# Two blocks on one core: the first two slabs of IN's second half of K in turns, and four visits of w_ada one chunk later

## What is computed

```python
c_act = jax.nn.silu(c)
mod = c_act @ w_ada[l] + b_ada[l]                      # 2048 x 12288
sh1, sc1, gt1, sh2, sc2, gt2 = jnp.split(mod, N_MOD, axis=-1)
h = modulate(rmsnorm(x, g_norm_mix[l]), sh1, sc1)      # h * (1 + scale) + shift
proj = h @ w_in[l]                                     # 2048 x 3072
xr, gr, xp = proj[..., :D_LRU], proj[..., D_LRU:2 * D_LRU], proj[..., 2 * D_LRU:]
```

## Time and profile before

| | |
|---|---|
| median of 3 runs | 2534.44 us (2533.34 to 2534.62) |
| the profiled execution | 2534.16 us, of which 2531.9 are its span |
| PE busy | 2494.3 us, 99% |
| DVE busy | 1833.2 us, 72% |
| ACT busy | 1182.2 us, 47% |
| granted clock of PE | 0.996 of full, mean |

### The profile page before, as it was taken

The page is one execution under the profiler, slowest core; times in us unless marked ns, Lnnn a source line. Parts: engine busy times, 40 slices in busy tenths (PEclk is TensorE's granted clock), DMA queues, the critical chain, the costliest instruction groups (busy, mean ns, idle before and its releaser), DMA issues.

```text
span 2531.9 us, 42099 instructions
## 1 busy us (share of the span) xinstructions
PE 2494.3 (99%) x15684; PEld 2173.4 (86%) x15684; DVE 1833.2 (72%) x2377; ACT 1182.2 (47%) x1442; POOL 17.6 (1%) x52
## 2 busy tenths in 40 slices
PE   7999999999999999999999999999999999999998
PEld 6888888888888888888888888888888888888887
DVE  5678989996556655787685665676788668875886
ACT  3355445544444444654454554455544444444444
POOL 0000000000000000000000000000000000000000
PEclk9999999999999999999999999999999999999999
DMA  9999978787666665566555555565555655565554
GB/s 392 410 375 362 371 261 276 248 330 240 187 187 187 190 205 170 180 207 192 181 167 174 159 184 190 182 195 189 180 193 184 196 178 182 196 197 181 186 172 127
DMA packets 165174, 554.68 MB, mean 219 GB/s; under 512 B 16560, under 2 KB 20656, under 8 KB 165056
## 3 DMA queue, kind: packets, MB, share of 16 engines
q1 hardware_dynamic: 163728, 549.85, 65.2%
q0 software_dynamic: 1328, 3.21, 0.4%
HBM read 550.37 MB, written 2.10 MB: 218 GB/s over the span
## 4 chain that ended last, share of the span: by engine, by line
PE 87%; DVE 7%; DMA 2%; issue 2%; ACT 2%; SPq 0%; DVEq 0%; ACTq 0%
PE ps L642 51%; PE ps L649 25%; PE ps L639 2%; DMA ride<-in_w_ada 2%; DVE split L1377 2%; PE pm L667 1%; DVE acc_ada L1443 1%; PE ps L646 1%; PE ps L622 1%; PE ps L623 1%; PE ps L624 1%; ACT split L1010 1%; DVE x_t L1543 0%; DVE val L1397 0%; DVE ssq L1461 0%
## 5 line engine op out<-in xcount | busy, mean ns | idle before, releaser
L1377 DVE TENSOR_TENSOR split<-raw,split 128x1024 fp32r<-128x1024 f32 (+1 forms) x864 | 1030.8, 1204 | 591.8 <-ACT split L1010 587.3
L1010 ACT ACTIVATE split<-raw 128x1024 fp32r<-128x1024 f32 (+1 forms) x864 | 897.0, 1044 | 1069.7 <-PE ps L649 940.5
L642 PE MATMUL ps<-h_s,split 128*128 128x512 f32 x3592 | 1134.2, 397 | 4.5 <-DVE h_s L1521 2.5
L649 PEld LDWEIGHTS ps<-h_s,split 128*128 128x128 f32 x3592 | 675.7, 188 | 159.9
L642 PE MATMUL ps<-mid_s,split 128*128 128x512 f32 x2336 | 735.0, 396 | 0.8 <-DVE split L1377 0.4
L649 PE MATMUL ps<-h_s,split 128*128 128x256 f32 x3592 | 706.5, 278 | 0.0
L642 PEld LDWEIGHTS ps<-h_s,split 128*128 128x128 f32 x3592 | 548.6, 189 | 9.3 <-issue 5.6
L649 PEld LDWEIGHTS ps<-mid_s,split 128*128 128x128 f32 x2336 | 438.8, 188 | 103.8
L649 PE MATMUL ps<-mid_s,split 128*128 128x256 f32 x2336 | 459.0, 278 | 0.0
L642 PEld LDWEIGHTS ps<-mid_s,split 128*128 128x128 f32 x2336 | 355.6, 189 | 4.7 <-issue 2.7
L1017 ACT ACTIVATE low<-ps 128x512 f32<-128x512 f32 x238 | 138.1, 580 | 22.3 <-PE ps L649 22.3
(11 more groups left out here) (285 smaller groups left out, 1482.9 us busy)
## 6 DMA issues: line engine op xcount, KB each, us to landing
raw<-in_w_in SPq DMA_DIRECT2D x224, 512.0 KB, 3.8
raw<-in_w_ffn_down SPq DMA_DIRECT2D x128, 512.0 KB, 4.2
ride<-in_w_ada SPq DMA_DIRECT2D x46, 1024.0 KB, 11.5
raw<-in_w_ffn_gate SPq DMA_DIRECT2D x88, 512.0 KB, 4.1
raw<-in_w_ffn_up SPq DMA_DIRECT2D x88, 512.0 KB, 4.3
raw<-in_w_ffn_a SPq DMA_DIRECT2D x88, 512.0 KB, 3.6
raw<-in_w_ffn_b SPq DMA_DIRECT2D x88, 512.0 KB, 4.5
raw<-in_w_out SPq DMA_DIRECT2D x64, 512.0 KB, 4.5
```

The source lines that it names most:

```text
L642: pe.matmul(ps[:, s, b, :], split[:, slot, k, 0, b * P:(b + 1) * P], acts[:, k0 + k, :, :].rearrange("p h t -> p (h t)"), start=start, sto ...
L649: mm = pe.matmul(ps[:, s, b, 0:T], split[:, slot, k, 1, b * P:(b + 1) * P], acts[:, k0 + k, 0, :], start=False, stop=stop)
L1010: act.activation(split[:, c, 0:kt, 0, :], raw[:, CHUNKS * s + c, 0:kt, :], ACT.Copy).then_inc(hi_ready, 1)
L1377: dve.tensor_tensor(split[:, c, 0:kt, 1, :], raw[:, CHUNKS * s + c, 0:kt, :], split[:, c, 0:kt, 0, :].bitcast(F32), ALU.subtract).then_inc ...
```

## The change

Three things change. `_early` swaps slab and quarter for the first four chunks of the second half: chunk 24 is quarter 2 of slab 0, 25 quarter 2 of slab 1, 26 quarter 3 of slab 0, 27 quarter 3 of slab 1. PE multiplies them so (`first_halves`), with both PSUM places open at once, and DVE's evacuation of slab 0 waits for 27 used chunks, not 26. In `_rides` the visits after chunks 16, 18, 20 and 21 come after 17, 19, 21 and 22, and with them their loads, DVE's and ACT's steps on unit 3, and nothing else.

```diff
 def _early(G):
...
     slab, c = divmod(G - HALF_CHUNKS, 2)
+    if slab < 2:
+        slab, c = c, slab
     return slab, 2 + c
...
-    at = [at for at in (2, 4, 6, 8, 9, 11, 13, 15, 16, 18, 20, 21) for _ in range(2)]
+    at = [at for at in (2, 4, 6, 8, 9, 11, 13, 15, 17, 19, 21, 22) for _ in range(2)]
...
+        def first_halves():
+
+            for i in range(4):
+                G, q, c = HALF_CHUNKS + i, i % 2, i // 2
+                if c == 0:
+                    pe.wait_ge(evacuated, HALF_CHUNKS + q - 1)
+                multiply_narrow(G, G % RING, q, h_s, KT * (2 + c), KT, c == 0, c == 1, ready=KT * (2 + c) if q == 0 else None)
+                ride_along(G)
+
         def half_slab(q, after):
...
-                multiply_narrow(G, G % RING, q % 2, h_s, KT * (2 + c), KT, c == 0, c == 1, ready=KT * (2 + c) if q == 0 else None)
+                multiply_narrow(G, G % RING, q % 2, h_s, KT * (2 + c), KT, c == 0, c == 1)
...
-        for q in range(IN_SLABS):
+        first_halves()
+        for q in range(2, IN_SLABS):
...
-            evacuate_narrow(HALF_CHUNKS + q, q % 2, partial(q) if q < 8 else val[:, q % 2, :, :], partial(q), HALF_CHUNKS + 2 * q + 2)
+            evacuate_narrow(HALF_CHUNKS + q, q % 2, partial(q) if q < 8 else val[:, q % 2, :, :], partial(q), HALF_CHUNKS + (3 if q == 0 else 2 * q + 2))
```

## The result

The changed kernel takes 2537.24 us (median of 20 runs, 2536.3 to 2537.78), the kernel before 2533.86 us in the same job (20 runs, 2533.04 to 2534.73): a ratio of 1.0013, with a 95% interval of 1.0007 to 1.0019. It is slower by 3.4 us, which is under the 0.2% that I set as a difference. The prediction was 2534.8 us in a range of 2532.2 to 2536.8: the sign was right, but the loss was some six times what I worked out, and the time lies 0.4 us outside the range.

What follows compares the result with a forecast made beforehand. PE bounds the kernel, busy 2494.3 of 2531.9 us. The visits' 1.67 us gain turns into 0.5 us lost through POOL's loads: 2534.16 + 0.5 = 2534.7; predicted 2534.8 us, range 2532.2 to 2536.8.

Steps and rivals of the forecast that it cites:

- Part 1: Visits of pieces 24 to 31 one chunk later: 1.67 us won on PE if nothing else is in the queue.
- Rival B: POOL's loads come later after chunk 21 or hit a piece less; piece 31 lands at 126.6: 2532.5 us, chance 0.22.
- A: The forecast: POOL's small loads make piece 31 2.2 us late, at 128.8; 0.5 us lost, 2534.7 us, chance 0.55.
- D: PE's clock falls to its 1.2 GHz level around the wait for piece 31: up to 5.1 us more, 2539.8, chance 0.03.
- The other estimate: With a first byte after about 1 us, POOL's small loads delay piece 30 as well: 1.4 us lost, not 0.5.
- Part 2: Slabs 0 and 1 of the second half in turns: spares chunk 25 coming 1.2 us too early for h; no gain alone.
- C: DVE's later evacuation of slab 0 loses its 1.1 us of cover: 1 to 2 us more, 2536.2 us, chance 0.12.
- E: PE's shift is lost later, as DVE's full stretch from 262 us starts when it started: 2534.2 us, chance 0.08.

## Why the prediction was wrong

**Part 1's times: right.** The waits (0.56 us for 0.73 at piece 25, none at 27 and 29), the visits and POOL's first load came as worked out, and the gain of 1.67 us without POOL's loads was measured at 1.64.

**Rival B is out, A's mechanism is right, and its size was short.** Piece 31 was hit by POOL's loads. I put it at 2.2 us late by the row of a chunk at its distance; it was 3.2 (landed at 129.8, due at 126.6), within the bounds that I had kept (0 and 3.3). That is 1.0 us more on PE. The row taken was one of a steep rise, in which a chunk gets from 0.2 to 3.4 us late within 2.5 us, and it was a chunk's and not a piece's.

**D is the step that failed.** I had the mechanism and its place, but gave it a chance of 0.03 and nothing in the sum, while my own upper bound for piece 31 was 3.3 us. The argument against it was one wait of 2.36 us without a fall. The runs show that this was the luck of one execution: at the same place the clock fell after 2.33 and 2.15 us of waiting, in two kernels that differ from the kernel before only later, and at other places after 2.38 and 1.88. So the point from which I let it decide ("if piece 31 comes more than some 3 us late") had no row behind it and was too high. In the changed kernel PE stood still from 125.65 us on and the clock fell at 127.70 by its records, 2.05 us later; in this execution the 3.05 us that I forecast would have been enough. The Trainium skill's rule that I cited ("TensorE: Matmul & The Clock Gate", "Why this matters for your kernels") was that idle gaps between bursts of matmuls bring the lower clock back. The changed kernel's trace agrees with it (0.50 behind a wait of 4.21 us), and one earlier wait that did not fall was no ground to set it aside. Its size I had as up to 5.1 us, from a low stretch of 10 us; the low stretch was 6.8 us, of which PE would have waited 2.1 anyway, and it cost 2.0 to 2.15 us.

The sum: 0.53 us as predicted, 1.06 from the larger lateness (129.86 for 128.8), 2.01 from the clock (from piece 31's start to chunk 24 6.04 us, not 4.03), together 3.60 of the 3.66 us by which chunk 24 was later. The range had the first two, up to the bound of 3.3 us, but not the third on top of them.

In the changed kernel `ident` landed 4.9 us after its issue (5.9 before), which again speaks for a late start of POOL's loads. The other estimate, 1.4 us lost, supposed an early start and had no working in the prediction; nothing rests on it.

**Part 2, C and E.** Part 2 cost nothing and is worth 1.3 us, as worked out (1.2). C did not come: chunk 26 starts at 141.66 us without a wait, h's last blocks having begun at 139.62; DVE evacuates slab 0 at 145.56, and the gates begin at 152.22, 3.66 us later than before, exactly the shift at chunk 24. E did not come either: the shift was still 3.65 us at chunk 48 (239.06 for 235.41) and 3.2 at chunk 80, the first of the feed-forward (340.78 for 337.57), behind DVE's full stretch.

## What to carry to other kernels

When a step is moved, look for everything that its new time sets off on other queues: here one visit less in the way let PE release five small loads 3.8 us earlier, into a full queue, just ahead of the one piece that PE was waiting for. A wait that grows may cost the clock as well, so the price of the two belongs in one case; a single execution in which the clock held does not show that it will hold in the next. And a load that gives up its place must be followed to every engine that handles it: twice here the chunk that paid for an earlier piece held up DVE's evacuation behind its conversion.

## What was not expected of the hardware

- The clock after a wait is not the same from execution to execution: at the visit after chunk 16 it stayed at 1.00 through 2.36 us of waiting in one, and fell to 0.50 for 3.4 us after 2.33 and 2.15 us in two others. Waits of 0.3 to 1.2 us for pieces, and two of 1.3 us for h, showed no fall in these traces.
- Low stretches came in lengths of 3.4, 6.8 and 10.2 us in the clock's records. The one near 335 us, which every execution here has, was 6.8 us long in some and 10.2 in others; it may be part of the spread of 1 to 2 us between runs of one kernel, but each kernel here but one has a single profiled execution, so that is not shown.
- A kernel can have two times a few us apart with no change in its program: in the kernel before with POOL's loads earlier, an early fall of the clock put off the small loads by 1.6 us, and the piece that they had held up by 3 us in the other execution came through almost on time.
